# Prompt attention of a two-layer decoder step: values held in TensorE, four heads' probabilities moved past them

## The reference, cut to what matters

```python
logits = einsum('btgrd,btkgd->btgrk', qg, k_sel)        # 8 heads, 2 key/value groups, head width 128
logits = where(valid, logits, -inf)
p = softmax(logits, axis=-1)
o = einsum('btgrk,btkgd->btgrd', p, v_sel)
y = x + (o * silu(gate)) @ w_out                        # 1024 x 1024 output projection
```

## Time and profile before

| | |
|---|---|
| time, median of 3 runs | 1778.81 us (1779.67, 1774.89, 1778.81) |
| profiled execution, span from first to last instruction | 1776.7 us; no other time of it is shown |
| busy over the span: TensorE | 1689.8 us (95%), 10109 matmul passes |
| VectorE | 1262.0 us (71%) |
| ScalarE | 764.5 us (43%) |
| GpSimd | 533.1 us (30%) |
| mean granted TensorE clock | 0.976 of 2.4 GHz |

### The profile page before, as it was taken

One profiled execution on the slowest core, in us unless ns is written; L12 is line 12 of the kernel. 1 busy time (PEld: TensorE's weight loads), 2 busy tenths in 40 slices (PEclk: granted clock), 3 DMA queues, 4 the chain that ended last, 5 costly groups with the idle time before them and its releaser, 6 DMA issues. The chain is left out here.

```text
span 1776.7 us, 26877 instructions
## 1 busy us (share of the span) xinstructions
PE 1689.8 (95%) x10109; PEld 967.8 (54%) x10109; DVE 1262.0 (71%) x2081; ACT 764.5 (43%) x1812; POOL 533.1 (30%) x632
## 2 busy tenths in 40 slices
PE   8999999999998999998999999999998879999999
PEld 6534434444446566665444544444435866777775
DVE  2399969999996798992696554646454677777773
ACT  2357867874225343333211242232212656554551
POOL 2502200100112111000225777777722512222320
PEclk9999999999999999999999999999998869999999
DMA  7406440110026111202413455555689444434321
GB/s 231 136 1 220 160 146 15 40 49 30 30 79 253 65 48 58 98 24 80 127 44 101 128 172 172 168 171 166 198 283 338 126 150 102 130 100 109 94 58 59
DMA packets 164024, 211.35 MB, mean 119 GB/s; under 512 B 45576, under 2 KB 114720, under 8 KB 163872
## 3 DMA queue, kind: packets, MB, share of 16 engines
q1 hardware_dynamic: 121912, 153.62, 26.6%
q0 software_dynamic: 16896, 50.35, 9.2%
q10 hardware_dynamic: 25088, 5.66, 1.5%
HBM read 165.86 MB, written 43.74 MB: 118 GB/s over the span
## 5 line engine op out<-in xcount | busy, mean ns | idle before, releaser
L1578 POOL DMA_INDIRECT scores<-in_cache_k,rowidx x128 | 135.6, 1059 | 39.5 <-issue 36.7
L2211 POOL DMA_INDIRECT home<-in_cache_v,rowidx x128 | 132.9, 1038 | 39.0 <-issue 38.4
L1189 DVE MAX8 top_v<-scores 128x8 f32<-128x4100 f32 x32 | 141.6, 4427 | 0.4
L1191 DVE FIND_INDEX8 top_i<-top_v,scores 128x8 uint32<-128x4100 f32 x32 | 141.5, 4422 | 0.0
L1193 DVE MATCH_REPLACE8 scores<-top_v,scores 128x4100 f32<-128x4100 f32 x32 | 141.2, 4413 | 0.0
L186 ACT ACTIVATE junk_topk_h<-key_mask,bs_cand 128x640 f32<-128x640 f32 (+1 forms) x104 | 102.0, 983 | 32.0 <-DVE bs_cand L196 25.8
L1399 PE MATMUL ring<-w_out_att,ogT_blk 128*128 128x512 f32 x256 | 113.0, 600 | 1.0 <-ACT ogT_blk L1432 0.9
L965 PE MATMUL acc<-w_out_att,xnT 128*128 128x512 f32 x256 | 112.7, 593 | 0.0
L965 PE MATMUL acc<-w_kvq,xnT 128*128 128x512 f32 x256 | 111.4, 593 | 0.0
L3600 PE MATMUL PY<-home,ogT_dn 128*128 128x512 f32 x224 | 101.8, 596 | 0.0
L1432 ACT COPY pT_blk<-tp_blk 128x512 f32<-128x512 f32 (+3 forms) x96 | 43.2, 486 | 121.4 <-PE tp_blk L1369 121.2
(11 more groups left out here) (560 smaller groups left out, 3598.4 us busy)
## 6 DMA issues: line engine op xcount, KB each, us to landing
S_s<-in_dn_w_in SPq DMA_DIRECT2D x24, 512.0 KB, 4.8
qkv_d<-y_ch SPq DMA_DIRECT2D x24, 512.0 KB, 3.7
qkv_t<-qkv_d SPq DMA_DIRECT2D x8, 1536.0 KB, 8.0
home<-in_dn_w_in SPq DMA_DIRECT2D x5, 2048.0 KB, 13.9
x<-in_x_all SPq DMA_DIRECT2D x8, 512.0 KB, 3.5
w_kvq<-in_att_w_in SPq DMA_DIRECT2D x2, 2048.0 KB, 13.0
qT_d<-qTb SPq DMA_DIRECT2D x8, 512.0 KB, 2.7
gate_d<-sgate SPq DMA_DIRECT2D x8, 512.0 KB, 3.1
```

The lines of the kernel that those rows point to most:

```text
L1189: link(dve.max(v, scores[:]))
L1191: dve.max_index(top_i[:, 8 * r:8 * r + 8], v, scores[:])
L1578: pool.indirect_dma_start(rows[:, j % KR, c, :], None, ck, bass.IndirectOffsetOnAxis(ap=idx[:, c, query(j):query(j) + 1], axis=0)).then_in ...
L2211: pool.indirect_dma_start(vg[:, j % VR, c, :], None, cv, bass.IndirectOffsetOnAxis(ap=rowidx[:, c, query(j):query(j) + 1], axis=0)).then_i ...
```

## The change

- In `weigh` the values are stationary now. The probabilities of the four heads of a group lie beside each other in `pT` and move together, 512 columns a pass, at the steps with `h = 0` and `h = 4`. The result comes out turned. The last group is weighed in two pieces, three heads and one.
- `pT` lies in memory of `xnT`, which is free at that time; its layout is by key tile, then head.
- The gate is multiplied by the reciprocal row sums on GpSimd, then turned by TensorE (`turn_gate`, four tiles, at steps 2 and 6) and copied by ScalarE to `gT`.
- ScalarE copies the turned output, four heads in one instruction, to `ogT`; GpSimd multiplies it there by `gT` (`gated_out`). For the last half VectorE makes both products.
- `out_proj` waits for each half of `ogT` only where it first reads it.
- VectorE adds the residual before the mask of its step, and `inverse` stands at `h = 0` and `h = 4`.
- `span` has other weights.

```diff
+        NG, LAST = NB * G, NB * G - 1
-        pT = sb("pT_blk", [P, 2, NB, P])
+        pT = keep["xnT"][:].rearrange("p k n -> p (k n)")[:, 0:2 * NB * GRP * P].rearrange("p (u k h q) -> p u k h q", u=2, k=NB, h=GRP)
+        gT = sb("gT_blk", [P, H, P])
...
-                    sp.wait_ge(og_ok, 2 * (i + 1))
+                    sp.wait_ge(tp_done, turned(("g", 2 * i + 1)))
                     load_gate(i + 2)
...
             def gated(k):
-                pool.wait_ge(o_taken, 4 * k + 4)
-                link(pool.tensor_tensor(v, v, gate[:, i % 2, 512 * u:512 * (u + 1)], ALU.mult))
                 pool.wait_ge(ri_ok, k + 1)
-                pool.tensor_tensor(v, v, ri[:, hh].unsqueeze(2).broadcast_to([P, 4, HD]), ALU.mult).then_inc(og_ok, 1)
+                pool.tensor_tensor(v, v, ri[:, 4 * u:4 * u + 4].unsqueeze(2).broadcast_to([P, 4, HD]), ALU.mult).then_inc(gr_ok, 1)
+            def gated_out(k):
+                u = k % 2
+                v = ogT[:, 4 * u:4 * u + 4, :]
+                pool.wait_ge(oc_ok, k + 1)
+                pool.wait_ge(tp_evac, turned(("g", k)))
+                pool.tensor_tensor(v, v, gT[:, 4 * u:4 * u + 4, :], ALU.mult).then_inc(og_ok, 1)
...
-            def weigh(hc):
...
-                for k in range(tiles(hc)):
-                    ins = pe.matmul(ops[:, hc % 2, 0:HD], pT[:, hc % 2, k, :], v_nat[:, k + 1, g * HD:(g + 1) * HD],
+            def weigh(k, bank, first, last):
+                i, g = divmod(k, G)
+                pe.wait_ge(tp_evac, turned(("p", 4 * k + last - 1)))
+                if bank >= 2:
+                    pe.wait_ge(oc_ok, bank - 1)
+                for j in range(i + 1):
+                    ins = pe.matmul(ops[:, bank % 2, first * P:last * P], v_nat[:, j + 1, g * HD:(g + 1) * HD],
+                                    pT[:, k % 2, j, first:last, :].rearrange("p h q -> p (h q)"), start=(j == 0), stop=(j == i))
...
+            def turn_gate(k):
...
+                turn(("g", k), gate[:, i % 2, 512 * u:512 * (u + 1)], GRP)
...
-                if i >= 1 and h == OG_AT:
-                    turn_out(i - 1)
+                if hc >= 6 and hc % 4 == 2:
+                    turn_gate((hc - 6) // 4)
                 if i >= 1 and h == Y_AT:
                     out_proj(i - 1)
                 turn_probs(hc)
-                if hc >= 1:
-                    weigh(hc - 1)
-            weigh(NH - 1)
-            turn_out(NB - 1)
+                if hc >= 4 and hc % 4 == 0:
+                    weigh(hc // 4 - 1, hc // 4 - 1, 0, GRP)
+            weigh(LAST, LAST, 0, GRP - 1)
+            turn_gate(LAST)
+            weigh(LAST, NG, GRP - 1, GRP)
             out_proj(NB - 1)
...
             exps(0)
             for hc in range(NH):
-                if i >= 1 and h == OG_AT:
-                    out_turned(i - 1)
+                if hc >= 6 and hc % 4 == 2:
+                    gate_turned((hc - 6) // 4)
                 if hc + 1 < NH:
                     exps(hc + 1)
...
-                if hc >= 2:
-                    take_out(hc - 2)
-                evac(("p", hc), tiles(hc), pT[:, hc % 2, :, :])
+                if hc >= 5 and hc % 4 == 1:
+                    take_out(hc // 4 - 1)
+                probs_turned(hc)
...
-                return (0.5 * i + 0.28 if i >= 3 and hc < NH - 3 else 0.0) + (13.9 if i >= 1 and h == Y_AT else 0.0)
+                rest = 0.2 * i + (0.88 * (i if h == 0 else i + 1) if h % GRP == 0 else 0.0)
+                return (rest if i >= 2 and hc < NH - 3 else 0.0) + (13.9 if i >= 1 and h == Y_AT else 0.0)
...
             masked(1)
             for hc in range(NH):
+                if i >= 1 and h == RES_AT:
+                    residual(i - 1)
                 if hc + 2 < NH:
                     masked(hc + 2)
-                if i >= 1 and h == RES_AT:
-                    residual(i - 1)
...
+                if hc >= 4 and hc % 4 == 0:
+                    inverse(hc // 4 - 1)
...
+            inverse(LAST)
+            last_out(LAST, 0, GRP - 1)
+            last_out(NG, GRP - 1, GRP)
```

More of the change, by code:

```diff
@@ L1211, in sem @@
             return new_sem(nc, env, name)
-        q, gate, x, og = (keep["first_blk"][k] for k in ("q", "gate", "x", "og"))
+        q, gate, x = (keep["first_blk"][k] for k in ("q", "gate", "x"))
         lm = sb("lm", [P, LR, SEQ])
@@ L1239, in prompt_attend @@
         o_done = sem("ob_done")
[L1240 to L1241 removed]
+        gr_ok, gr_last, og_ok, og_last, oc_ok, ri_ok = (sem(t) for t in ("gr_ok", "gr_last", "og_ok", "og_last", "oc_ok", "ri_ok"))
         pch = sem("pool_chain_pa")
[L1243 removed]
         y_out = [env["stores"][f"y1_out{u}"] for u in range(2)]
@@ L1253, in prompt_attend @@
                 uses.append(("l", s + 2))
-            if (h == OG_AT and 1 <= i) or s == NH:
-                turns.append(("og", i - 1 if s < NH else NB - 1))
+            if s >= 6 and s % 4 == 2:
+                turns.append(("g", (s - 6) // 4))
             if (h == Y_AT and 1 <= i) or s == NH:
@@ L1260, in prompt_attend @@
         at = {u: n for n, u in enumerate(uses)}
+        turns.append(("g", LAST))
         tp_at, n = {}, 0
@@ L1269, in turned @@
         def turned(t):
-            return tp_at[t] + (2 if t[0] == "og" else (tiles(t[1]) + 3) // 4)
+            return tp_at[t] + (1 if t[0] == "g" else (tiles(t[1]) + 3) // 4)
         block = ctx.enter_context(nc.Block())
@@ L1336, in rms @@
                 pool.tensor_tensor(rss[:, t, :], ss[:, t, :], mhalf[:], ALU.pow).then_inc(rs_ok, 1)
-            for k in range(LAST_HALF):
+            for k in range(LAST):
                 gated(k)
+                gated_out(k)
                 if k == 2 * SQUARE_AT + 2:
@@ L1398, in out_proj @@
                     for h in range(H):
+                        if a == 0 and h % GRP == 0:
+                            if 2 * i + h // GRP < LAST:
+                                pe.wait_ge(og_ok, 2 * i + h // GRP + 1)
+                            else:
+                                pe.wait_ge(og_last, 1)
+                        if a == 0 and h == H - 1 and i == NB - 1:
+                            pe.wait_ge(og_last, 2)
                         ins = pe.matmul(dst[:, a:a + 512], ogT[:, h, :], wo[:, h, a:a + 512], start=(h == 0), stop=(h == H - 1))
@@ L1430, in evac, with probs_turned, take_out, gate_turned @@
                     act.wait_ge(tp_done, b + 1)
[L1431 to L1435, removed]
+                    act.copy(dst[:, n:n + m, :], tpb[:, b % 2, 0:m, :]).then_inc(tp_evac, 1)
+            def probs_turned(hc):
+                k = hc // GRP
+                if k >= 2 and hc % GRP == 0:
+                    act.wait_ge(o_done, k - 1)
+                evac(("p", hc), tiles(hc), pT[:, k % 2, :, hc % GRP, :])
+            def take_out(k):
+                i, u = divmod(k, 2)
+                act.wait_ge(o_done, k + 1)
                 if i >= 1:
                     act.wait_ge(ring_done, at["y", i - 1] + 1)
[L1438 to L1445, removed]
+                act.copy(ogT[:, 4 * u:4 * u + 4, :].rearrange("p h q -> p (h q)"), ops[:, k % 2, :]).then_inc(oc_ok, 1)
+            def gate_turned(k):
+                u = k % 2
+                if k >= 2:
+                    act.wait_ge(og_ok, k - 1)
+                evac(("g", k), GRP, gT[:, 4 * u:4 * u + 4, :])
             exps(0)
@@ L1483, in inverse, with last_out @@
             def inverse(k):
-                u = k % 2
+                i, u = divmod(k, 2)
                 dve.wait_ge(exp_ok, 4 * k + 4)
                 if k >= 2:
[L1487 to L1499, removed]
+                    dve.wait_ge(gr_ok, k - 1)
+                ins = dve.reciprocal(ri[:, 4 * u:4 * u + 4], rs[:, 4 * u:4 * u + 4])
+                if k < LAST:
+                    ins.then_inc(ri_ok, 1)
+                    return
+                link(ins)
+                dve.wait_ge(g_in[i % 2], 16 * (i // 2 + 1))
+                v = gate[:, i % 2, 512 * u:512 * (u + 1)].rearrange("p (h e) -> p h e", e=HD)
+                dve.tensor_tensor(v, v, ri[:, 4 * u:4 * u + 4].unsqueeze(2).broadcast_to([P, 4, HD]), ALU.mult).then_inc(gr_last, 1)
+            def last_out(bank, first, last):
+                i, u = divmod(LAST, 2)
+                dve.wait_ge(tp_evac, turned(("g", LAST)))
+                dve.wait_ge(o_done, bank + 1)
+                dve.wait_ge(ring_done, at["y", i - 1] + 1)
+                h = slice(4 * u + first, 4 * u + last)
+                dve.tensor_tensor(ogT[:, h, :], ops[:, bank % 2, first * P:last * P].rearrange("p (h q) -> p h q", q=P), gT[:, h, :], ALU.mult).then_inc(og_last, 1)
             def residual(i):
```

34 lines of the change are left out of this document (9 added, 25 removed).

## The result

The changed kernel takes **1783.38 us** (median of 20 runs, 1778.16 to 1791.34), the kernel before, on the same chip, 1778.55 (20 runs, 1769.49 to 1785.06): ratio **1.0037, 95% interval 1.0023 to 1.0050**. The medians are 4.8 us apart, 0.27%; the ratio says 0.37%, some 6.6 us. So the kernel is slower by an amount clear of zero and about as large as the 0.3% that counted as no change. The profiled execution took 1786.55 us, 1.75 more than its span of 1784.8; that of before had a span of 1776.7.

What follows compares the result with a forecast made beforehand. TensorE sets the pace, VectorE alone comes near; the prediction sums TensorE's waits. Terms -2.6 + 0.8 + 3.7 - 1.7 - 2.5 + 3.4 = +1.1 us: span 1777.8, median 1779.9, range 1768 to 1788.

Steps and rivals of the forecast that it cites:

- A: Weighing with values stationary, four heads moved together: 61.9 us in place of 64.5, so -2.6 us.
- the rival that they bind: Weight loads between short weighing passes cost what the busy column suggests: -11.5 us there, time 1771; chance 0.05.
- the -38: Weight loads between short weighing passes bind, by the Trainium skill's figures: about -38 us, time 1744.
- B: Waits for the residual beside the projection, with passes added there: 7.5 us against 6.7 before, so +0.8 us.
- C: Gate turned instead of output, twice a block: 8.5 us lost at turns waiting for ScalarE, so +3.7 us.
- D: Top-k passes away from the projection's step: fewer TensorE waits for masks and exps behind a pass, -1.7 us.
- E: Tail: last projection's first half waits for nothing, half clock goes, 1.2 us lost at the last turns; -2.5 us.
- F: TensorE's clock halved after the long waits of blocks 2 and 5: 1.7 us each, +3.4 us, between 0 and 5.
- Cost at nothing: Work on ScalarE, GpSimd's products, SP's loads and strided probabilities in the stage: taken to add no time.
- the waits go: Rival: residual placed first and passes fit, so the projection's waits vanish: -13.5 us, 1765, half of that 1772; chance 0.20.
- Light heads uncover the clock: Rival: short waits in steps without weighing halve the clock five more times: 8.5 us more, 1788; chance 0.25.

Runs made afterwards that it cites:

- the second of before: The kernel before, no edit, profiled once more: 1769.88 us, stage 296.6, scan 390.0.
- the two padded runs: Tiny unused matmuls added at the stage's end: 26 in the changed kernel, 1778.31 us (ratio 1.0020); 38 in the kernel before, 1780.69 us (1.0026).

## Why the prediction was right and where it was wrong

The forecast was 1779.9 with a range of 1768 to 1788; 1783.4 lies inside. It called for no measurable change; measured is a small loss that is clear of zero, 4.8 us by the medians. In the profiled pair the stage did what the sum said, in part by luck (below). What failed is a step that the prediction never wrote down: that a stage with unchanged code takes unchanged time.

- **A, right.** 160 weighing passes took 62.0 us from start to start; the sum had 61.9. The weight loads saved nothing more: the rival that they bind (-11.5) did not come. Nor did the -38 that follows from the figures of the Trainium skill ("TensorE: Matmul & The Clock Gate", section "Back-to-back issue gap"): the stage's weighing fell by 2.5 us, from the 64.5 reckoned for before to 62.0.
- **B, right.** Waits in blocks 1 to 6, refill included: 0, 2.36, 1.27, 0.17, 3.49 and 0, against 0, 2.5, 1.3, 0.2, 3.5 and 0. Setting VectorE's work against TensorE's, block by block, is what carried this. The two runs that move the residual back show the gain that the added passes hid: 9 us in after, 5 to 8 of the stage in before.
- **C, right in size** (about 8 us of 8.5), and its cover as well: with the gate moved, the stage fell by 5.7, not 8, since about 2 came back as waits for masks in block 6 and 1 as waits for GpSimd in blocks 0 and 1.
- **D, slightly low:** block 6's two passes cost 1.26 for 0.95.
- **E, partly.** `out_proj` of block 7 starts with no wait and the tail shows no half clock; its turns cost 1.8 for 1.2: head 63's bank was late by the 1.2 foreseen, and the gate's turn ahead of it waited another 0.5 for a bank. The 1.75 credited for the half clock was no fixed price of the tail: of the five traces that have the old tail one shows it, the one that the prediction read.
- **F, wrong in block 2.** Two half clocks were charged at 3.4; one came, for 1.5. The wait of 2.36 us left the clock at 1.00, that of 3.49 did not. In other runs waits of 2.6 and 2.9 us near block 2 were followed by half clock, so the prediction's bounds (0 to 5) were right and its single value was not.
- **Not seen: the squares.** Two instructions on ScalarE, placed by step number, lost their cover when weighing left light steps: 1.9 us. Cost at nothing was argued for ScalarE as a whole ("under half busy"), and that was the wrong unit.

The stage's sum stands, corrected: -0.2 (B), -0.5 (C), +0.3 (D), +0.6 (E), -1.9 (F), +1.9 (squares) against +1.1 makes +1.3; measured +1.2. Two errors of 1.9 cancelled, and the sum is met only against the execution that it was read from: against the second of before the stage costs 3 to 4 us.

- **Not seen: the scan.** +8.1 in the profiled pair. The trace of before had it in sight: stops of 1.6 us that wait for "issue" among matmuls of 0.016, and 81 packets of q8 for a list that the change shortens by 871. Nothing there says which way the borders move, but a term of either sign, as large as the 5.1 us of stops in before, belonged in the range. By the two padded runs it is some 3 to 5 us of the times. With the stage's +1 to +4, less the 1 to 2 that after wins between stage and scan in the two profiled pairs, that covers the measured 4.8 to 6.6; the runs don't separate the parts to a microsecond. The Trainium skill ("Runtime: NRT & Kernel Launch", section "Instruction fetch mechanics") says that crossing a 16 KiB boundary is mostly hidden. Here that holds for most borders: in the scan of after 36 packets arrive and seven stops stand, among the smallest matmuls.

Of the rivals, "the waits go" failed for the reason given there, block 5's five passes. "Light heads uncover the clock" did not come: one half clock behind the stage's start, not five. The waits of 0.2 to 0.6 in the light steps left no mark on the clock.

What stays open: why the packet comes late (around the longest stop, 1440 to 1450 us, the data queue q1 took 80% of the time of all sixteen DMA engines, but this was not tested); and whether another shift would bring the version with the residual first below 1765.87, which was not tried.

## What to carry to other kernels

Add up waits by starts and by stage, and for each moved wait set the two engines' work between the same two events against each other: that gave each wait of B here to a tenth or two. Before a change of many instructions look where the long burst engine waits for "issue": the length of its list can cost or give several microseconds in code that nobody touched, so compare stages before crediting the edit, and shift the list once to see. And when one stretch of cover is moved away, list each instruction on every engine that stood under it, by step, not the engine's mean load; the best piece of this change was exchanging two statements, and the rest of it consumed what that gave.

## What the runs showed of the hardware

- TensorE stops for 0.9 to 3.6 us inside bursts of 32 x 32 matmuls with no semaphore involved; 104 or 152 instructions put in 550 us earlier moved the stops, in both directions (2.5 against 10.6 us, 11.8 against 5.1). Every stop ended 1.2 to 1.6 us after a 16 KB packet of the instruction queue had landed.
- The same wait is not always followed by the same clock: the 3.3 us behind block 5 by 3.4 us near half clock in two executions of after, and by 6.8 where only the squares were moved; the two waits of 1.0 in the tail of before by half clock at once in one trace, and by none in the four others with this tail.
